# A fused two-block layer on one core: blocks masked by chunk, other panels around the scatter, own buffers for one level, and GpSimd held back behind two norms

## What is computed

```python
h = h + 0.5 * rmsnorm(swiglu(rmsnorm(h, n[0]), ffn1_wi, ffn1_wo), n[1])
h = h + rmsnorm(hybrid_mixer(rmsnorm(h, n[2]), ...), n[3])
h = h + 0.5 * rmsnorm(swiglu(rmsnorm(h, n[4]), ffn2_wi, ffn2_wo), n[5])
```

```python
m = where(strict, einsum('bhnck,bhnsk->bhncs', k_beta, k) * decay_mask, 0)
t = triangular_solve(eye + m, eye, left_side=True, lower=True, unit_diagonal=True)
u, w = t @ v_beta, t @ (k_beta * exp(gc)[..., None])
```

## Time and profile before

| | us |
|---|---|
| median of 3 runs | 1062.21 (1061.55 to 1063.92) |
| the profiled execution | 1060.77 |
| its span in the profile | 1059.0 |
| TensorE busy | 1015.0 |
| weight loads busy | 991.7 |
| GpSimd busy | 778.1 |
| VectorE busy | 567.8 |
| ScalarE busy | 477.4 |
| mean granted clock of TensorE | 0.984 of 2.4 GHz |

### The profile page before, as it was taken

The page is one execution under the profiler, slowest core; times in us unless marked ns, Lnnn a source line. Parts: engine busy times, 40 slices in busy tenths (PEclk is TensorE's granted clock), DMA queues, the critical chain, the costliest instruction groups (busy, mean ns, idle before and its releaser), DMA issues.

```text
span 1059.0 us, 21628 instructions
## 1 busy us (share of the span) xinstructions
PE 1015.0 (96%) x8190; PEld 991.7 (94%) x8190; DVE 567.8 (54%) x1020; ACT 477.4 (45%) x708; POOL 778.1 (73%) x599
## 2 busy tenths in 40 slices
PE   7999999999999999999999889989999999999995
PEld 6899999999999999999889789999999889999995
DVE  4315994457644444735876363446656764444334
ACT  6244324456554444335556424423246365545441
POOL 2396776657989989995688635646539949999993
PEclk9999999999999999999999799989999999999998
DMA  9363434443656555554443123434315626655561
GB/s 345 116 188 119 123 108 135 125 129 119 179 170 194 168 173 169 168 181 138 140 143 116 41 80 100 131 91 138 101 61 179 217 83 188 198 188 176 183 182 56
DMA packets 48298, 154.62 MB, mean 146 GB/s; under 512 B 6028, under 2 KB 11156, under 8 KB 48232
## 3 DMA queue, kind: packets, MB, share of 16 engines
q1 hardware_dynamic: 46080, 151.31, 46.1%
q10 hardware_dynamic: 2152, 2.38, 0.7%
HBM read 151.57 MB, written 2.10 MB: 145 GB/s over the span
## 4 chain that ended last, share of the span: by engine, by line
PE 73%; DVE 12%; POOL 8%; ACT 3%; issue 3%; DMA 0%; SPq 0%; DVEq 0%; ACTq 0%; POOLq 0%
PE panel L1606 56%; POOL wlo L607 6%; PE panel L1653 3%; DVE qkv L1321 1%; PE panel L1701 1%; PE aux L1750 1%; DVE qkv L1326 1%; DVE q L1196 1%; PE panel L1689 1%; DVE s L1175 1%; DVE k L1197 1%; DVE qkv L1317 1%; PE aux L1982 1%; PE aux L1992 1%; PE aux L1945 1%
## 5 line engine op out<-in xcount | busy, mean ns | idle before, releaser
L607 POOL TENSOR_TENSOR wlo<-raw,whi 128x512 fp32r<-128x512 f32 x552 | 749.1, 1388 | 257.8 <-ACT whi L695 256.6
L1606 PE MATMUL panel<-xh,whi 128*128 128x256 f32 (+1 forms) x1440 | 420.2, 292 | 4.0 <-DVE xl L1024 2.0
L1606 PE MATMUL panel<-xh,wlo 128*128 128x256 f32 (+1 forms) x1440 | 411.7, 286 | 0.0
L1606 PE MATMUL panel<-xl,whi 128*128 128x256 f32 (+1 forms) x1440 | 410.9, 285 | 0.0
L695 ACT ACTIVATE whi<-raw 128x1024 fp32r<-128x1024 f32 x276 | 289.3, 1053 | 192.8 <-PE panel L1606 167.5
L1606 PEld LDWEIGHTS panel<-xh,whi 128*128 128x128 f32 x1440 | 274.1, 190 | 6.3 <-issue 5.2
L1606 PEld LDWEIGHTS panel<-xl,whi 128*128 128x128 f32 x1440 | 273.5, 190 | 0.6
L1606 PEld LDWEIGHTS panel<-xh,wlo 128*128 128x128 f32 x1440 | 274.0, 190 | 0.0
L1606 PE MATMUL panel<-hh,wlo 128*128 128x272 f32 (+1 forms) x352 | 100.6, 286 | 0.0
L1606 PE MATMUL panel<-hh,whi 128*128 128x272 f32 (+1 forms) x352 | 100.3, 285 | 0.0
L1606 PE MATMUL panel<-hl,whi 128*128 128x272 f32 (+1 forms) x352 | 100.0, 284 | 0.0
(11 more groups left out here) (310 smaller groups left out, 1612.4 us busy)
## 6 DMA issues: line engine op xcount, KB each, us to landing
raw<-in_panels SPq DMA_DIRECT2D x228, 512.0 KB, 3.5
raw<-in_down SPq DMA_DIRECT2D x32, 448.0 KB, 3.2
raw<-in_down SPq DMA_DIRECT2D x16, 512.0 KB, 3.5
memk<-in_mem_panels SPq DMA_DIRECT2D x4, 512.0 KB, 7.5
memv<-in_mem_panels SPq DMA_DIRECT2D x4, 512.0 KB, 13.4
memx<-in_mem SPq DMA_DIRECT2D x4, 256.0 KB, 5.1
h<-in_x SPq DMA_DIRECT2D x1, 1024.0 KB, 8.1
spill<-h ACTq DMA_DIRECT2D x1, 1024.0 KB, 4.7
```

What stands on the lines that cost most here:

```text
L607: ins = nc.gpsimd.tensor_tensor(wlo[:, slot, half], raw[:, slot, half], whi[:, slot, half].bitcast(f32), ALU.subtract)
L1606: ins = M(bank[:, 0:w], wt[:, slot, P * t:P * t + P], x[:, kk, c0:c0 + w], start=first and m == 0 and n == 0, stop=last and m == len(pairs ...
```

## The change

Six things are changed.

1. `mask_blocks(c)` masks the two units of chunk c alone, 8 of 32 matrices, in four instructions. ScalarE does chunk 0 at the end of its work for chunk 1, and so on; only chunk 3 is left at the gather, where TensorE waits for 16 instead of 4 marks.
2. The rows of the inversion are dealt out 4, 4, then 2 at a time; the second gate panel stands behind the last `dft_out` instead of ahead of it; the second half of the branch stands behind the scatter.
3. The level of 34 has its own two buffers `aoff34`. Their first two contents are made behind the last `aoff` of the level of 17, and the others one step earlier than before.
4. GpSimd waits for all low halves (`split_low`) of the norm ahead of the mixer, and of the norm behind OUT2, before it makes the next panel's `wlo`. In each place that is one panel.
5. TensorE goes through OUT2's first two panels in two passes, tiles 0 to 5 of both, then 6 and 7 of both.
6. On ScalarE, at the end of the first block, the `whi` of the last panel ahead stands in front of the squares of tile 7 instead of behind them.

```diff
     beside = [("dft_out", 0), ("dft_in", 2), panels[1], ("dft_out", 1), ("dft_in", 3), panels[2],
-              ("dft_out", 2), panels[3], ("dft_out", 3)]
+              ("dft_out", 2), ("dft_out", 3), panels[3]]
+    row = 1
     for n, step in enumerate(beside):
-        steps += [step] + [("invert", r) for r in range(2 * n + 1, min(2 * n + 3, SUB))]
-    steps += panels[4:6] + [("scatter",)]
+        rows = 4 if n < 2 else 2
+        steps += [step] + [("invert", r) for r in range(row, min(row + rows, SUB))]
+        row += rows
+    steps += [panels[4], ("scatter",), panels[5]]
     panels = panels[6:]
...
         xm = at("xm", ar + 4896, [CH, 2, 4, CH])
+        aoff34 = at("aoff34", ar + 5440, [CH, 2, 4, CH])
         state = at("state", ar + 3264, [P, 2, 4, P])
...
             loop(UP + 24)
+            pool.wait_ge(split_low, 8 * SPLIT[5] + 8)
             for step in MIXER:
...
             ahead(OUT2_P + 7)
+            pool.wait_ge(split_low, 8 * SPLIT[7] + 8)
+            ahead(UP2_P)
             loop(PANELS - split[0] - (PANELS - split[0]) % RING)
...
                 A(xh[:, t, META:LEN], h[:, t, META:LEN], ACT.Identity, scale=first_gain[:, t:t + 1]).then_inc(split_high, 1)
+                if t == 7:
+                    ahead(UP1_P)
                 if t >= 4:
...
             first_tile(7)
-            ahead(UP1_P)
...
             act.dma_start(a["spill"], h[:, :, META:LEN]).then_inc(h_saved, 16)
+            def mask_blocks(c):
+                act.wait_ge(am_ready, 2 * c + 2)
+                for b in range(4):
+                    at_b = slice(SUB * b, SUB * b + SUB)
+                    A(amx[:, :, b, 8 * c:8 * c + 8].rearrange("i j m -> i m j"),
+                      am[:, 2 * c:2 * c + 2, :, at_b].rearrange("i u h j -> i (u h) j"),
+                      ACT.Identity, scale=block_of_row[:, b:b + 1]).then_inc(blocks_masked, 1)
...
                         A(dmat[:, d, 0], dmat[:, d, 0], ACT.Exp, scale=-1.0).then_inc(decay_ready, 1)
+                    if i:
+                        mask_blocks(i - 1)
                 if kind == "gather":
-                    act.wait_ge(am_ready, 8)
-                    for b in range(4):
-                        at_b = slice(SUB * b, SUB * b + SUB)
-                        A(amx[:, :, b, :].rearrange("i j m -> i m j"), am[:, :, :, at_b].rearrange("i u h j -> i (u h) j"),
-                          ACT.Identity, scale=block_of_row[:, b:b + 1]).then_inc(blocks_masked, 1)
+                    mask_blocks(NC - 1)
                 if kind == "scatter":
...
                     aux_wait(dve, AUX[("x17", u - 2)])
-                if level == 1:
-                    aux_wait(dve, AUX[("x17", 6 + u)] if u < 2 else AUX[("x34", u - 2)])
+                if level == 1 and u >= 2:
+                    aux_wait(dve, AUX[("x34", u - 2)])
                 if level == 0 and u == 0:
                     dve.wait_ge(am_ready, 8)
-                TT(aoff[:, u % 2], am[:, u], bc(lvl[:, level, :], 1, 4), ALU.mult).then_inc(aoff_ready, 1)
+                TT((aoff34 if level else aoff)[:, u % 2], am[:, u], bc(lvl[:, level, :], 1, 4), ALU.mult).then_inc(aoff_ready, 1)
...
                     part_of_a(0, i)
-                if step == ("u17", 7):
-                    part_of_a(1, 0)
-                if kind == "x34" and i < 7:
-                    part_of_a(1, i + 1)
+                    if i == 7:
+                        part_of_a(1, 0)
+                        part_of_a(1, 1)
+                if kind == "x34" and i < 6:
+                    part_of_a(1, i + 2)
                 if kind == "t17":
...
                     aux_open(n)
-                    pe.wait_ge(blocks_masked, 4)
+                    pe.wait_ge(blocks_masked, 4 * NC)
                     for j in range(SUB):
...
                     for hd in range(4):
-                        ins = M(bank[0:CH, CH * hd:CH * hd + CH], aoff[:, i % 2, hd, :], um[:, i, hd, :], start=True, stop=True)
+                        ins = M(bank[0:CH, CH * hd:CH * hd + CH], (aoff if kind == "x17" else aoff34)[:, i % 2, hd, :],
+                                um[:, i, hd, :], start=True, stop=True)
                     ins.then_inc(aux_full, 1)
...
                         ins.then_inc(aux_full, 1)
-            for i in range(8):
-                output(OUT2_O + i, OUT2_P + i, mgh, mgl, ROWS, each=(lambda kk: pe.wait_ge(mg_low, kk + 1)) if i == 0 else None)
+            for tiles in (range(0, 6), range(6, KT)):
+                for i in range(2):
+                    o, p = OUT2_O + i, OUT2_P + i
+                    if tiles[0] == 0:
+                        open_output(o, p)
+                    ins = products(pb[o % 4], p % RING, [(kk, kk) for kk in tiles], mgh, mgl, 0, ROWS, tiles[0] == 0,
+                                   tiles[0] == 6, lambda kk: pe.wait_ge(mg_low, kk + 1))
+                    if tiles[0] == 6:
+                        ins.then_inc(passed, 1)
+            for i in range(2, 8):
+                output(OUT2_O + i, OUT2_P + i, mgh, mgl, ROWS)
             norm_stat(6)
...
```

## The result

| | before | after |
|---|---|---|
| median, us | 1062.77 (1061.55 to 1063.92) | 1046.20 (1043.69 to 1049.21) |
| profiled execution, us (span) | 1060.77 (1059.0) | 1046.90 (1045.1) |
| mean granted clock | 0.984 | 0.988 |

The medians are over four runs each. The ratio is 0.9845 with a 95% interval of 0.9816 to 0.9875. 1047.5 was forecast, with 1042 to 1055.5 as the range.

What follows compares the result with a forecast made beforehand. TensorE, busy 1015.0 of 1059.0 us, sets the end; gains come from its waits and half-speed clock. Terms sum to 14.7, taking the profiled 1060.77 to 1046.1; plus 1.4 for the median gives 1047.5, range 1042 to 1055.5.

Steps and rivals of the forecast that it cites:

- 7, `whi` earlier: End of first block: moving ScalarE's `whi` ahead of two squares costs between 0 and 1.05 us, taken as 0.
- Part 1: Masks by chunk: the wait for `amx` goes, chunk 3 ends about 1.8 us later, the gather gains 1.3 (0 to 3.0).
- Part 2: Low clock at the gather: half of its 5.0 us cost is won back, 2.5 (0 to 5.0).
- the low clock only moves: Rival: waits go but low stretches turn up elsewhere; gain 7.6 us, 1054.6; chance 0.17.
- Part 3: Panels around the scatter: waits of 1.9 and 1.4 us go, a new 2.3 for `tbx` comes; net gain 1.0.
- The term for the clock, 0: Low stretch at 635.9, by the scatter: left as it is, 0 (gain of 1.5 to loss of 1.5).
- Part 4: Own buffers for the level of 34: the 3.3 us `aoff` wait and its low stretch go; gain 6.0 (3.0 to 6.3).
- The 0.3 left for `xm`: Level of 34: ScalarE's `xm`, behind the same convolution, is late next and leaves some 0.3 us of waiting.
- Part 5: OUT2 in two passes: 1.7 us of the `mgl` wait and 1.6 of low clock go; gain 3.3 (1.5 to 3.8).
- Part 6: GpSimd rests in both norms: gain 0.25 us at the first, 0.35 at the second; 0.6 (0 to 1.0).
- The bound of 1.3 that I took from one product: Second norm: by the SBUF page, the gain lies between nothing and the whole of GpSimd's last product, 1.3 us.
- The signs I named: `aoff`, `mgl` waits at most 0.6; no 0.50 stretch near 690, 827; `tbx` wait about 2.3; `amx` wait below 0.5.

Runs made afterwards that it cites:

- r_after: The changed kernel run again with nothing edited: 1047.04 us, ratio 0.9847 against the kernel before.
- u_whi: Changed kernel, but ScalarE rounds the first block's last panel behind the norm's last tile again: 1047.50 us, ratio 0.9853.
- u_rest: Changed kernel, but GpSimd does not rest and makes the two panels behind the norms' tiles at once again: 1051.83 us, ratio 0.9889.
- u_x34: Changed kernel, but the level of 34 shares the level of 17's two buffers again, made behind the convolution's instructions: 1052.68 us, ratio 0.9902.
- u_out2: Changed kernel, but OUT2's eight outputs go one after the other again, the first waiting for tiles 6 and 7: 1049.32 us, ratio 0.9872.
- n_tbx: Changed kernel, with ScalarE masking the inverses at the last dft_out, ahead of the gate's sigmoid and `whi`: 1044.20 us, ratio 0.9820.
- u_order: Changed kernel, but with the order of panels and inversion rows round the scatter as before: 1048.51 us, ratio 0.9876.
- n_fillc: n_both, with six added products of ones in each of TensorE's two waits in chunk 3: 1043.78 us, ratio 0.9811.
- n_both: n_tbx, with the masks of chunks 1 and 2 moved to the end of chunk 3: 1044.19 us, ratio 0.9810.
- r_before: The kernel before run again with nothing edited, for one more trace: 1062.68 us.

## Why the prediction was right, point by point

Measured is the mean of the two traces of before less the mean of the six that have the changed code up to there (after, r_after, u_whi, u_rest, u_x34, u_out2; for parts 4 and 5 the five without that part's undoing; at the second norm the four without u_rest and u_out2).

| part | predicted | measured |
|---|---|---|
| 1, up to the gather | 1.3 | 89.17 - 87.91 = 1.3 |
| 2, gather to the second dft_out | 2.5 | 15.32 - 13.63 = 1.7 |
| 3, on to the first x17 | 1.0 | 28.20 - 27.16 = 1.0 |
| 4, x34 to OUT2 | 6.0 | 134.55 - 128.32 = 6.2 |
| 5, OUT2 | 3.3 | 26.74 - 23.17 = 3.6 |
| 6, the norms | 0.6 | 0.15 at the first, 210.58 - 210.93 = -0.35 at the second |
| 7, `whi` earlier | 0 | 0 |
| sum | 14.7 | 13.6 |

**Part 1.** The last chunk's four masks, in the timeline of ScalarE, take a third of the row, as forecast (1.4):

```profile
592.93 1.45 ACT L893 ACTIVATE amx<-am,sel 68x136 f32<-68x136 f32 x4 [1.63 <-POOL am L658]
```

Chunk 3's products end 2.1 later in the first pair of traces, 0.6 of it there by 508; behind the cut at 508 they end at 80.5 in the mean of the six and at 78.6 in that of before, 1.8 later, as worked out. The way there is the one forecast as well: the masks of chunks 0 and 1 push chunk 2's copy of `kt` from 0.74 to 1.98 behind the start of its transposes and chunk 3's from 5.11 to 7.24. TensorE waits for no `amx`, and the gain is what was worked out. That the sum came out to a tenth is partly luck: its six values run from 86.0 to 89.4.

**Part 2** was oversized, 2.5 for 1.7. The gather itself is at full speed in four of six traces and the stretch at 599 is 6.8 in the mean instead of 10.2, but the one at 585 is 6.8 in four of the six, where it was 3.4 before. The time at 0.50 from 508 to `x17` is 21.1 in the mean of the six and 18.8 in that of before. Here the rival "the low clock only moves" had it right in time, and the forecast only in place.

**Part 3.** The wait of 2.3 for `tbx` was 2.2, in the order forecast (sigmoid 0.42, `whi` 1.04, `tbx` 1.80), and n_tbx shows its cause. The term for the clock, 0, held too: the stretch is twice as long and makes the half panel behind the scatter 1.2 us dearer (2.72 against the 1.47 of one at full speed), and the panel behind that gives back 1.4 (3.01 against 4.36).

**Part 4** was right in both halves, and the clock went with the wait. The 0.3 left for `xm` did not come. **Part 5** was right in its wait, but undersized there (2.3 for 1.7, since the 0.5 that I left to wait did not come), and its clock's half is not sure (1.3 for 1.6), since u_out2 had the wait without the stretch.

**Part 6** failed as a step, though its sum was small. I took its worth from the kernel before, where GpSimd's row of products ends at 852.61, 0.5 behind the start of the pair in the earlier trace rows, and did not carry part 5 into it: with OUT2 3.6 us shorter TensorE and VectorE reach the norm that much earlier, and GpSimd, whose row of products is bound by itself, doesn't. Without the rest 3.3 us of its products lie on the norm (841.57 to 844.91) and cost 2.1. With it the row ends at 838.77, 0.5 behind the pair's start, and the pair takes 1.2, both as before. So the rest gains nothing against the kernel before, and keeps 2.1 of part 5's gain from being given back. That it was the arrival and not the pair's own cost that I had wrong is seen in u_out2, which has the rest without part 5: there GpSimd is idle when the pair starts, the pair takes 0.88, and the cut to the end is 210.29, 0.3 less than before, the 0.35 of the forecast. The -0.35 of the table lies ahead of the pair: TensorE stands still for 0.56 to 0.80 in front of its last products for the norm's sum of squares, where it was 0.38 before. It does so in u_rest too (0.79), so it isn't the rest; what makes it I did not test. The bound of 1.3 that I took from one product was too small.

**The signs I named.** No wait for `aoff` or `mgl`, no low stretch near 690 or 827, 2.2 after `tbx`, no wait for `amx`: all there. No wait of over 1 us is in a place where the kernel before has none, but for the one at the scatter that was named. Low rows that sum to as much as before: 17.1 and 23.9 in the two traces of the changed kernel (3.4 of the latter near 112, outside the table), 27.3 and 30.7 in those of before. The 10.2 that don't come back are the two stretches of parts 4 and 5.

**The medians** differ by 16.6 and 16.3, the profiled executions by 13.9 and 14.1. Of the 2.5 between, 1.3 is that the two profiled executions of before lay below its medians, and 1.1 that those of the changed kernel lay above its own. The parts that were undone cost 5.8 + 2.7 + 4.4 + 3.1 + 4.5 + 0.6 = 21.1 in ratios, more than the whole change; each is known to 3 or 4 us, part 6's worth rests on part 5, and how the clock reacts to each is not additive. What is open is which of these is behind the excess of u_order and u_rest over their traces. So it is luck in part that 1047.5 lies 1.3 from the median of 1046.20: the sum was 1.1 too large, mostly by parts 2 and 6, and those 2.5, which I did not foresee, more than made up for it.

## What to carry to other kernels

A part that lets one engine arrive earlier changes what the next part is worth: cost them in the order of time, with the backlog of every engine at the new time, not each against the trace of before. A wait's own name is only its last link: `dmat` was late for masks that stood further back in ScalarE's queue. An instruction in a queue is ahead of all that is written behind it, so look first for a late one that needs nothing from its neighbours (here `tbx`, 2.9 us for four moved lines). And where the clock is at its low level around sparse work, take several traces of the same code before a stretch is put down to an edit.

## What the runs showed of the chip

Identical products in the same order came under 17.1 to 27.3 us at 0.50 between 508 and `x17`, and took 126.5 to 131.7 us for it: 5 us, more than the range of most of the terms above. The page "TensorE: Matmul & The Clock Gate" of the Trainium skill (What's actually happening) says that what watches TensorE's activity runs free of the kernel, so that the point of a change shifts from run to run. The traces show the shift, with a larger effect than that page gives for a start from idle, half a microsecond either way; they do not show what makes it.

In or right behind the wait of 3.3 us for `aoff` the clock fell in three of three traces, and in none of the eleven without the wait. With the wait of 2.2 us for `tbx` one came at the scatter in all eight traces. Of the three with `tbx` moved ahead, which have no wait there, two have one too (n_tbx, n_fillc) and one has none (n_both); the kernel before, r_before and u_order, with 1.4 us of waiting behind the scatter instead, have theirs there. So the wait of 2.2 is not needed for it; what is, these runs do not show.
